# PEER experts: the U tiles of quarter 0 are multiplied beside the top-k, and their V tiles run alone after it

## What is computed

```python
qh = (xb @ w_q).reshape(tb, 8, 2, 128)
s = jnp.einsum('thsd,hskd->thsk', qh, sub_keys)      # 16 rows of 128 keys a token
sv, si = lax.top_k(s, 16)
cand = (sv[:, :, 0, :, None] + sv[:, :, 1, None, :]).reshape(tb, 8, 256)
cv, ci = lax.top_k(cand, 16)
eid = i1 * 128 + i2                                  # i1, i2: indices behind ci
gate = jax.nn.softmax(cv, axis=-1)
a = jnp.einsum('td,thkd->thk', xb, u_tab[eid])
coef = gate * jax.nn.gelu(a, approximate=False)
return jnp.einsum('thk,thkd->td', coef, v_tab[eid])
```

## Time and profile before

| | |
|---|---|
| median of three runs | 2887.89 us (2887.79 to 2890.28) |
| the profiled execution | 2890.28 us, its span 2890.3 us |
| PE, DVE, ACT, POOL busy | 86%, 67%, 35%, 16% |
| mean granted clock of PE | 0.919 |
| end of w_q to the first expert tile | 1073.2 to 1267.9 us |
| quarter 0's eight steps | 1267.9 to 1677.0 us |

### The profile page before, as it was taken

The page is one execution under the profiler, slowest core; times in us unless marked ns, Lnnn a source line. Parts: engine busy times, 40 slices in busy tenths (PEclk is TensorE's granted clock), DMA queues, the critical chain, the costliest instruction groups (busy, mean ns, idle before and its releaser), DMA issues.

```text
span 2890.3 us, 55547 instructions
## 1 busy us (share of the span) xinstructions
PE 2478.7 (86%) x21845; PEld 2339.2 (81%) x21845; DVE 1940.0 (67%) x2565; ACT 1022.2 (35%) x1156; POOL 473.0 (16%) x220
## 2 busy tenths in 40 slices
PE   6499995788669681269999999999999999999998
PEld 2199995555459681159999999999999999999998
DVE  0467665443186678987877878777787877766666
ACT  1166693111033330133333333333333333333333
POOL 0000001465120000551211212121121211000000
PEclk9699998899679895569999999999999999999999
DMA  9455543588557440015444444444544444445453
GB/s 381 195 182 182 176 172 123 214 322 312 177 204 250 158 145 0 0 59 176 161 161 162 174 162 162 176 161 161 176 159 163 162 174 161 176 175 185 177 176 131
DMA packets 71439, 500.31 MB, mean 173 GB/s; under 512 B 8132, under 2 KB 8396, under 8 KB 14320
## 3 DMA queue, kind: packets, MB, share of 16 engines
q1 hardware_dynamic: 64368, 465.38, 44.4%
q0 software_dynamic: 6912, 32.50, 3.4%
HBM read 483.51 MB, written 14.35 MB: 172 GB/s over the span
## 4 chain that ended last, share of the span: by engine, by line
PE 81%; DVE 10%; DMA 4%; issue 3%; ACT 1%; POOL 1%; DVEq 0%; SPq 0%; ACTq 0%; POOLq 0%
PE ps L391 78%; DVE sb L1102 6%; DMA sb<-in_w_ada 3%; PE ps L429 2%; DVE sb L1108 1%; DVE sb L1105 1%; DMA sb<-rows_dram 0%; DVE sb L1551 0%; DVE sb L1501 0%; DVE sb L1498 0%; POOL sb L1692 0%; DVE sb L1499 0%; ACT sb L854 0%; DVE sb L1497 0%; DVE sb L1500 0%
## 5 line engine op out<-in xcount | busy, mean ns | idle before, releaser
L391 PEld LDWEIGHTS ps<-sb,sb 128*128 128x128 f32 (+1 forms) x20888 | 2298.3, 178 | 370.9 <-issue 245.7
L391 PE MATMUL ps<-sb,sb 128*128 128x264 f32 (+4 forms) x20888 | 2340.9, 273 | 286.2 <-DVE sb L1102 82.0
L1102 DVE TENSOR_TENSOR sb<-sb,sb 128x2048 fp32r<-128x2048 f32 (+12 forms) x1065 | 1360.1, 1312 | 466.0 <-ACT sb L854 320.4
L854 ACT CAST sb<-sb 128x2048 fp32r<-128x2048 f32 x340 | 650.9, 1915 | 536.1 <-PE ps L391 536.1
L1692 POOL TENSOR_TENSOR sb<-sb,sb 128x1056 bf16<-128x1056 bf16 (+3 forms) x157 | 427.7, 2731 | 1281.2 <-DVE sb L1102 1212.7
L1102 DVE TENSOR_TENSOR sb<-sb,ps 128x264 f32<-128x264 f32 (+2 forms) x577 | 253.3, 451 | 125.6 <-PE ps L391 101.2
L1066 ACT ACTIVATE sb<-ps 128x264 f32<-128x264 f32 x128 | 50.1, 391 | 463.9 <-PE ps L391 463.9
L429 PE MATMUL ps<-sb,sb 128*32 128x512 f32 x768 | 118.7, 716 | 33.6 <-DMA sb<-in_w_ada 22.7
L1037 ACT COPY sb<-ps 128x352 f32 x96 | 82.3, 857 | 127.8 <-PE ps L391 127.8
L1102 DVE TENSOR_TENSOR sb<-ps,sb 128x256 f32<-128x256 f32 (+6 forms) x45 | 13.5, 327 | 155.6 <-PE ps L391 149.7
L1108 DVE SCALAR_TENSOR_TENSOR sb<-sb,sb,sb 128x288 f32<-128x288 f32 (+3 forms) x220 | 95.1, 461 | 22.2 <-DMA sb<-v_dram 4.1
(11 more groups left out here) (127 smaller groups left out, 479.5 us busy)
## 6 DMA issues: line engine op xcount, KB each, us to landing
sb<-in_peer_u SPq DMA_DIRECT2D x128, 1024.0 KB, 4.8
sb<-in_peer_v SPq DMA_DIRECT2D x128, 1024.0 KB, 4.9
sb<-in_w_ada SPq DMA_DIRECT2D x96, 1024.0 KB, 7.7
sb<-in_w_in SPq DMA_DIRECT2D x52, 1024.0 KB, 4.8
sb<-in_w_out SPq DMA_DIRECT2D x16, 1024.0 KB, 5.0
sb<-in_w_q SPq DMA_DIRECT2D x16, 1024.0 KB, 4.8
sb<-rows_dram POOLq DMA_DIRECT2D x1, 4096.0 KB, 12.3
sb<-in_state_ssd POOLq DMA_DIRECT2D x8, 512.0 KB, 5.9
```

The costliest lines, as they stand in the source:

```text
L391: return pe.matmul(out, l, r, start=start, stop=stop)
L854: act.copy(whi[:, slot % 2], wring[:, slot]).then_inc(sem("hi_ready"), 1)
L1102: return dve.tensor_tensor(out, x, y, op)
```

## The change

Quarter 0 is done in two stretches. In the first its 32 U tiles (U0) run one after the other, each right behind the last; ACT's GELU writes each into `A0`, which lies where the first half of `G` was. The top-k, the turns and the 24 gate groups of quarter 0 stand between them, at places that the constants AT_... and GROUPS_AFTER give (after which U tile PE does what). The order is now prompt tile 1, prompt tile 2, sample. The Exp has its own place in ACT's queue (`weigh`), four, two and one tile ahead of `finish`. POOL makes the low parts of U tiles 1 to 21 (POOL_LOWS = 22), DVE those from 22 on. In the second stretch DVE multiplies the stored rows by their gates, four rows in one instruction (`raw_coef`), ACT rounds them (`coef_high`), DVE subtracts (`coef_low`), and eight groups of four V tiles follow, with quarter 1's gate groups behind the second, third and fourth V tile of each. Quarters 1 to 3 are as before. SP loads 32 U tiles and then 32 V tiles first. Some semaphores of the mixer are merged with others that are raised at the same place (dA_ready, xd_ready, qk_ready, rv0_ready).

```diff
@@ constants @@
-EARLY = 8
+U0 = QE
+AT_SCORES, AT_TURN1, AT_TURN2, AT_PAIR, AT_TURN0 = 2, 9, 18, 19, 21
+GROUPS_AFTER = {12: 1, 13: 1, 14: 1, 15: 1, 16: 1, 17: 1,
+                22: 2, 23: 2, 24: 2, 25: 2, 26: 2, 27: 2, 28: 2, 29: 2, 30: 1, 31: 1}
+POOL_LOWS = 22
@@ PE @@
+            for u in range(U0):
+                pe.wait_ge(sem("gelu_done"), u + 1)
+                if u < 2:
+                    pe.wait_ge(sem("q_ready"), N_Q + u + 1)
+                tile(ps[:, u % 2, 0:T], u % 2, L_E + u, hTh, hTl)
+                if u == AT_SCORES:
+                    sample_scores()
+                if u == AT_TURN1:
+                    turn(1)
+                if u == AT_TURN2:
+                    turn(2)
+                if u == AT_PAIR:
+                    sample_pairs()
+                if u == AT_TURN0:
+                    sample_turn()
+                for g in groups_after(u):
+                    gate_group(g, g % 2, 2)
             pe.wait_ge(sem("g_copied"), NG + 2)
...
-            with pe.Fori(0, 12) as i2:
+            with pe.Fori(0, 4) as i2:
+                for k in range(2):
+                    v_tiles(i2 * 2 + k, i2 * (2 * SLOTS) + (L_E + U0 + SLOTS * k), chis[k],
+                            lambda e: A0l[:, bass.ds(i2 * (2 * SLOTS) + (SLOTS * k + e), 1), :].rearrange(
+                                "p o t -> p (o t)"),
+                            (3 * k, 3 * k + 1, 3 * k + 2), i2 * 6 + NG)
+            with pe.Fori(4, 12) as i2:
@@ ACT @@
+            for u in range(U0):
+                early_high(u + 1)
+                act.wait_ge(gemm_done, T_U + u + 1)
+                act.activation(A0[:, u, :], ps[:, u % 2, 0:T], ACT.Gelu).then_inc(sem("gelu_done"), 1)
+                if u == AT_TURN1 - 4:
+                    weigh(1, 0)
+                if u == AT_TURN1:
+                    finish(1, 0)
+                if u == AT_TURN2 - 2:
+                    weigh(2, 1)
...
+                for g in groups_after(u):
+                    gate_copy(g, g % 2, QE, g * GT, 2)
@@ DVE @@
-            prompt(2, sv_2, siu_2, (lambda: gate_parts(0, P, 6), early(0, 1, 2), early(3, 4), early(5, 6, 7)))
+            prompt(2, sv_2, siu_2, (lambda: None, lambda: None, lambda: gate_parts(0, P, 3), early(0, 1)),
+                   (early(2), early(3)))
+            dve.wait_ge(sem("score_ps"), N_Q + 1 + SLOTS)
+            top16([(ps[:, 4, 0:128], sv_s[:, 0, :], siu_s[:, 0, :], work_s)])
...
+            for u in range(POOL_LOWS, U0):
+                early(*groups_after(u))()
+                low(L_E + u + 1, (u + 1) % SLOTS)
...
+            def v0_step(i, k, n, t0, last=False):
+                for q in range(4):
+                    if q < 3:
+                        g = 3 * k + q
+                        one_hots(n + g, g % 2, 1, t0 + g * GT)
+                    elif not last:
+                        coef_low(i + 1, 1 - k)
+                    low(i * SLOTS + (L_E + U0 + q + 1), (q + 1) % SLOTS)
+                    accumulate(i, q)
+            raw_coef(0, 1)
+            coef_low(0, 0)
+            raw_coef(2, 3, 4, 5, 6, 7)
@@ POOL @@
+            pool.wait_ge(sem("lo_ready"), L_E + 1)
+            for m in range(1, U0 + 1):
+                if m < POOL_LOWS:
+                    pool.wait_ge(sem("hi_ready"), L_E + m + 1)
+                    tt(wlo[:, m % 2], wring[:, m % SLOTS], whi_f[:, m % 2], ALU.subtract
+                       ).then_inc(sem("lo_ready"), 1)
+                for g in groups_after(m - 1):
...
+                    gate_rows(g, g % 2, g * GT)
```

More of the change, by code:

```diff
@@ L44, with groups_after @@
 NG = T // GT
-EARLY = 8
 QE = 32
 GDN_STEPS = 12
+U0 = QE
[3 more added lines that the diff above has]
+POOL_LOWS = 22
+def groups_after(u):
+    first = sum(n for at, n in GROUPS_AFTER.items() if at < u)
+    return range(first, first + GROUPS_AFTER.get(u, 0))
+assert sum(GROUPS_AFTER.values()) == NG
 SLOTS = 4
@@ L279, in build @@
         chi, chi_f = take_r(SLOTS, T)
+        clo_off = left[0]
         clo, _ = take_r(SLOTS, T)
@@ L308, in build @@
         assert left[0] <= xT_off
+        work_s = view(sqb_off + 512, 128)
         qT = acc
+        left[0] = acc_off
+        cand = take(8, 256)
+        oh = take(128, 16)
+        assert left[0] <= acc_off + KT * T
+        chis = (chi, view(clo_off, SLOTS, T, of=F32R))
+        chis_f = tuple(v.bitcast(F32) for v in chis)
         block = ctx.enter_context(nc.Block())
@@ new lines, in coef_high, with v0_step @@
+            def coef_high(i, k):
+                for e in range(SLOTS):
+                    if e == 0:
+                        act.wait_ge(sem("raw_coef"), i + 1)
+                    act.copy(chis[k][:, e, :], A0[:, bass.ds(i * SLOTS + e, 1), :].rearrange("p o t -> p (o t)")
+                             ).then_inc(sem("coef_hi"), 1)
+            early_high(U0 + 1)
+            coef_high(0, 0)
+            coef_high(1, 1)
+            act.wait_ge(sem("raw_coef"), 8)
+            def v0_step(i, k, last=False, ahead=True):
+                for q in range(SLOTS):
+                    act.wait_ge(sem("v_done"), i * KT + (4 * q + 5))
+                    if not (last and q == SLOTS - 1):
+                        high((q + 2) % SLOTS,
+                             i * 16 + (T_U // SLOTS * 16 + U0 // SLOTS * 16 + 16 + 16 * ((q + 2) // SLOTS)), None)
+                    if q:
+                        g = 3 * k + q - 1
+                        gate_copy(i * 3 + (NG + q - 1), g % 2, QE, i * (3 * GT) + (q - 1) * GT)
+                if ahead:
+                    act.wait_ge(sem("v_done"), i * KT + (KT + 1))
+                    coef_high(i + 2, k)
@@ L1061, in expert_step @@
+            with act.Fori(0, 3) as i2:
+                for k in range(2):
+                    v0_step(i2 * 2 + k, k)
+            v0_step(6, 0, last=False, ahead=False)
+            v0_step(7, 1, last=True, ahead=False)
             def expert_step(i, groups, g0, quarter, t0, end=False):
@@ L1576, in prompt @@
                 si4 = sif[0:n].rearrange("p (h s) k -> p h s k", s=2)
-                candidates(t, n, 8, lambda side: sv4[:, :, side, :], lambda side: si4[:, :, side, :], between)
+                candidates(t, t - 1, n, 8, lambda side: sv4[:, :, side, :], lambda side: si4[:, :, side, :],
+                           between, sides)
                 dve.sem_inc(sem("top_done"), 1)
@@ L1613, in split @@
+            with dve.Fori(0, 3) as i2:
+                for k in range(2):
+                    v0_step(i2 * 2 + k, k, i2 * 6 + NG, i2 * (6 * GT))
+            v0_step(6, 0, 18 + NG, 18 * GT)
+            v0_step(7, 1, 18 + NG, 18 * GT, last=True)
             def split(i, j):
                 low(i * (2 * SLOTS) + (L_E + j), j % SLOTS)
-            with dve.Fori(EARLY // 2, NG // 2) as i:
-                for b in range(2):
-                    one_hots(i * 2 + b, b, 0, i * (2 * GT) + b * GT)
```

217 lines of the change are left out of this document (118 added, 99 removed).

## The result

The changed kernel takes 2805.2 us (median of four runs, 2802.55 to 2814.19) where the kernel before takes 2888.0 (2887.79 to 2890.28): a ratio of 0.971, 95% interval 0.969 to 0.973. Predicted were 2807. The profiled execution takes 2802.55, its span is 2801.0.

What follows compares the result with a forecast made beforehand. First stretch bound by DVE's chain, second by a full TensorE; overlapped, DVE and POOL taking turns set the pace. 86 us saved less 5 for cold clock took 2890.3 to 2809, median 2807; range 2765 to 2840.

Steps and rivals of the forecast that it cites:

- POOL's split: In U tiles 1 to 21, POOL's subtraction of 2048 floats was put at 4.5 us, between bounds of 3.5 and 4.74.
- PE's wait for turn(1): In the U stretch, PE would wait some 11.5 us for the top-k of prompt tile 1.
- group 0 done: In the U stretch, the first gate group would be done at 1174.5 us, 101.3 after U tile 0 starts.
- first pair of groups done: Behind U tile 22, the first two groups, late by memset and gate_parts, would end at 1278 us.
- V step: In the V stretch, three gated tiles of 7.4 us and a fourth of 5.2 on DVE make 27.4 a step.
- 5 for the clock: Over quarter 0, 5 us were set against the saving of 86 for tiles restarting below full clock after a wait.
- the clock falls for good from tile 10 to 21: Rival, U stretch: half clock makes a tile take 11.6 us, adding 34 for a total of 2841; chance 0.14.
- half of the waits vanish: Rival, U stretch: DVE and POOL get along better, halving the waits charged to the top-k; 2765 to 2787 us, chance 0.15.
- No lock: Rival, U stretch: POOL's dense subtraction doesn't exclude DVE, V starts 72 us earlier; 2735 us in all, chance 0.06.
- The V stretch at 8.5 a gated tile: Rival, V stretch: low and one-hots blocked twice a tile, 8.5 us each, adding 27 for 2834; chance 0.11.
- A POOL split above 8 us: Rival, U stretch: splits with fp32r output use up the gain of 81 us at 8.4 each; slower than before, chance 0.05.
- Quarters 1 to 3 and the tail are untouched: Behind quarter 0, the forecast counted no change in time for the remaining quarters and the tail.

Runs made afterwards that it cites:

- E9: The kernel before, unedited, profiled once more: 2890.99 us, of which 1212.1 from the mark to the end.
- E10: The changed kernel, unedited, profiled once more: 2805.53 us, of which 1204.3 from the mark to the end.
- E1: Changed kernel with POOL's splits of U tiles 1 to 21 cut to 1024 of 2048 floats: 2791.69 us profiled against 2802.55.
- E5: Changed kernel without overlap: top-k and all 24 groups ahead of U tile 0, splits after the first on DVE; 2901.09 us profiled against 2802.55.
- E2: Changed kernel with prompt tile 2's Exp moved from behind GELU 16 to behind GELU 13: first to last GELU 272.3 us against 279.5; profiled 2810.03.
- E8: Changed kernel with turns and groups reordered, gate rows on DVE and eight POOL splits on DVE: 2766.3 us, ratio 0.955 to the kernel before.
- E3: Changed kernel with gate rows of groups 6 to 23 (U stretch) multiplied by DVE instead of POOL: 2805.42 us profiled, first to last GELU 269.9 against 279.5.
- E4: Changed kernel with quarter 1's gate rows (V stretch) multiplied by DVE instead of POOL: 2794.01 us profiled, last GELU to the mark 227.5 against 238.2.

## Why the prediction was right, and where it wasn't

**The stretch that it costed.** From the start of U tile 0 to the mark the kernel before has 1678.0 - 1073.2 = 604.8, the changed one 1601.0 - 1077.35 = 523.7. That is 81.1 saved; 81 were predicted. (To the first GELU of step 8 it is 85.4, by the 4.2 us at the seam that E9 and E10 show.) By its steps, counted from U tile 0:

| step | predicted | measured |
|---|---|---|
| POOL's split | 4.5 | 4.60 |
| top-k of tile 1 done | 72.8 | 71.0 |
| PE's wait for turn(1) | 11.5 | 8.9 |
| group 0 done | 101.3 | 97.5 |
| tile 18 ends | 170.8 | 169.9 |
| first pair of groups done | 204.8 | 205.0 |
| tiles 22 to 29, each | 9.65 | 9.67 |
| U tiles end | 285.8 | 286.2 |
| first one-hots of the V stretch | 297.8 | 297.8 |
| V step | 27.4 | 27.86 |
| mark | 518.8, with 5 for the clock 523.8 | 523.7 |

The mechanism was right, and E1 shows it by the length of the holds, E5 by the whole. Rows of 8 elements at 1.92 us in the old trace were enough to see it, and the 4.5 taken between the two bounds for a split that no row had was 0.1 off. In the changed kernel, under a split of 4.60 us on POOL, the first of the sixteen copies is held for 4.1 and a cast for 4.4, each with a single input. DVE's reads from PSUM do not wait, as the prediction has it. Beside the split from 1078.78 to 1083.38 two MAX8 take 0.50 (1080.58), as two do ahead of it (1077.56), and a FIND_INDEX8 takes 0.29. Four sums that read PSUM take 1.45 (1379.36) within a row product of POOL (1375.92 to 1381.27), as they do without one.

**Sizes that were off, and met.** Up to group 5 the sum ran 2 us late (164.8 against 162.8): too much for the splits in front of turn(1) and for group 0. Two later terms were too low and made it good: tile 18 restarts cold (group and tile 8.1, the granted clock 0.57 from 1228.93 to 1232.93), and from the sample's last product to the first pair of groups DVE needs 16.8, memset and gate_parts included, where I had 15. The Exp behind GELU 16 was in the sum; E2 prices it at 7.3.

In the V stretch one term was too low. The sum starts the steady run with DVE's first one-hots at 1371, 297.8 us behind U tile 0, and that is where they are (1375.19). From there to the mark it had 221, and measured are 225.8. 3.7 of the 4.8 are the steps at 27.86 instead of 27.4: the fourth tile of a step takes 6.1 instead of 5.2, since DVE's four sums wait 0.4 for PE there and then, each behind its product, take 1.9 instead of 1.45. Of the last 1.1 us, 0.8 are DVE's waits for PE in V tile 1, which runs at half clock until 1386.0 (0.50 from 1379.85 on).

So the 5 us set down for the clock were needed, but at most 1 of them for the clock, and this part of the agreement is luck. V tile 0 does run cold and takes 8.3 us (second row; the first is group 0's):

```profile
1173.85:1177.85 4.00, 4.00 (x47) 4.00 (x48) 3.75 (x7) 2.52 (x2) 0.33 (x1) 0.51 0.09 35
...
1367.40:1371.40 4.00, 4.00 (x18) 4.00 (x19) 4.00 (x6) 1.23 (x4) 0.00 (x0) 0.50 0.01 2
```

Yet V tile 0 holds nothing up. It ends at 1375.7, and V tile 1, at 1379.85, waits for DVE, which works without a break from 1366.8 to the sums of V tile 0:

```profile
1368.18 7.10 DVE L1209 TENSOR_TENSOR sb<-sb 128x1056 f32<-128x1056 f32 x6
1375.19 4.26 DVE L1209 TENSOR_TENSOR sb<-sb,sb 128x352 bf16<-128x352 f32 x3
...
1379.36 1.45 DVE L1209 TENSOR_TENSOR sb<-sb,ps 128x264 f32<-128x264 f32 x4
```

In the U stretch a restart cost PE 1.5 us (a group and a tile take 8.3, warm 6.8). The next group was waited for in any case, so most of it lay beneath DVE's chain; no run took it away by itself.

**Rivals.** That the clock falls for good from tile 10 to 21 did not happen: 0.78 over the stage, with a wait followed by some 4 us at 0.51 (the row from 1173.85 above) and full clock behind (1.00 from 1177.85 to 1181.85). That half of the waits vanish did not happen either: 8.9 of the 11.5 in front of turn(1) stood. No lock: excluded by E1 and the held copies. The V stretch at 8.5 a gated tile: 7.30. A POOL split above 8 us: 4.60. The lower end of the range, 2765, was called that rival's middle; it is its lower edge (2765 to 2787).

**What it did not cost.** "Quarters 1 to 3 and the tail are untouched" was wrong as a statement on time: in the profiled pair U tile 0 came 4.2 us later and the part behind the mark was 12.3 shorter. -81.1 + 4.2 - 12.3 = -89.2, and the spans differ by 89.3. So the profiled execution came 6.5 us below the 2809 predicted for it, in the second profile 3.5. Over the medians the saving is 82.8, and that 2807 lies so near to 2805.2 owes something to luck: terms that the sum left out pull both ways. Of the shorter part, 4.2 belong to the seam at step 8; the rest is PE's clock and gap at the turn of its loop, as E9 and E10 show, without a cause for the gap. The upstream time is open too: the last copy of Q stands at 1070.8 and 1072.1 in the two profiles of before and between 1075.0 and 1092.9 in the ten others, and no experiment was aimed at it.

## What to carry to other kernels

Before work is moved beside a stage that looks half idle, sum the instructions of DVE and POOL that can't run at the same time, their length times their number, and look for short copies whose recorded length is many times their own (here 1.92 us for 0.17): that is where the stage is already held. Where the two exclude one another, what counts is how long an operation keeps the other engine out, and not which of the two is busier: a split took 4.60 us on POOL and 2.29 on DVE, and taking eight of them back won 11 us (E8); the gate rows on DVE won 10 to 11 us in each stretch (E3, E4). And compare two such kernels from mark to mark within the trace, for totals hide changes of 10 us; check with the engine that sets the pace that the mark stands at the same place of its work, for here it was 4 us off.

## What the runs showed of the hardware that I had not expected

- A POOL subtraction of 2048 floats takes 4.60 us, of 1024 floats 2.40: 2.15 ns an element and 0.2 fixed. By these two lengths, cutting a split in two would cost 0.2 us; no run did it.
- One POOL split held products, copies and casts of DVE alike, with one input or two; MAX8, FIND_INDEX8, MATCH_REPLACE8 and TENSOR_REDUCE run at plain length beside it (2.71 for eight, 0.42, 0.41, 2.29 us).
- The turn of PE's loop costs clock in some passes: 24 of the 39 behind a gap of 1.74 us or more took 1.5 us longer, none of the 35 behind a shorter one; in E9 the first 10 us show 0.83 in a long pass and 1.00 in a short one.
